# Hybrid decoder layer on one core: norm row first, the first two token tiles ahead of the value weights and multiplied together, other small work moved

## The reference

```
hn   = rms_norm(x, g_pre_mix)
proj = hn @ w_in                      # 3078 columns: q, k, v of 6 MoBA heads, q, k, v of 6 forgetting heads,
                                      # 6 forget logits, 3 x 256 conv channels
moba = block attention, own 256-token block causal, plus past blocks, with a relative bias rel_bias[bucket(dist), head]
fox  = softmax(q k / 8 + cum[t] - cum[s], causal) v,   cum = cumsum(log_sigmoid(f_logit + b_f))
conv = gate_b * causal_conv3(gate_c * h)
mixed = concat(moba, fox, conv) @ w_out
x    = x + rms_norm(mixed, g_post_mix)
h2   = rms_norm(x, g_pre_ffn)
ff   = (silu(h2 @ w_gate) * (h2 @ w_up)) @ w_down      # inner width 2816
out  = x + rms_norm(ff, g_post_ffn)
```

## Time and profile before

| | us |
|---|---|
| three runs | 581.50, 582.97, 585.07 |
| their median | 582.97 |
| the profiled execution | 584.72 |
| its span, first to last instruction | 583.0 |
| TensorE busy (weight loads) | 572.5 (505.7) |
| VectorE, ScalarE, GpSimd busy | 471.9, 320.5, 117.3 |

### The profile page before, as it was taken

How to read it: one execution, slowest core, us unless ns; L and a number is a source line. 1 busy time by engine, 2 the same in 40 slices (tenths; PEclk the granted TensorE clock), 3 DMA queues, 4 the chain that set the end, 5 groups by cost and what they waited for, 6 DMA issues and landing times.

```text
span 583.0 us, 9681 instructions
## 1 busy us (share of the span) xinstructions
PE 572.5 (98%) x3380; PEld 505.7 (87%) x3380; DVE 471.9 (81%) x790; ACT 320.5 (55%) x539; POOL 117.3 (20%) x128
## 2 busy tenths in 40 slices
PE   8999999999999998999999999999999999999996
PEld 5988788888888887899999999999999988888884
DVE  2756888888787954589989888988898778898787
ACT  3644666566565643656454545545463565547752
POOL 3011100113220010000322324242323004344100
PEclk9999999999999998999999999999999999999999
DMA  8254343337312481122142323223231449999843
GB/s 331 74 180 147 98 117 112 92 108 232 107 43 78 144 319 73 63 83 74 72 146 73 128 87 131 85 79 137 81 135 72 144 154 285 262 213 206 161 144 144
DMA packets 27624, 78.92 MB, mean 135 GB/s; under 512 B 2972, under 2 KB 2972, under 8 KB 27594
## 3 DMA queue, kind: packets, MB, share of 16 engines
q1 hardware_dynamic: 18492, 56.92, 27.8%
q0 software_dynamic: 9008, 21.53, 16.8%
q10 hardware_dynamic: 94, 0.09, 0.0%
HBM read 71.16 MB, written 4.22 MB: 129 GB/s over the span
## 4 chain that ended last, share of the span: by engine, by line
PE 91%; DVE 4%; ACT 2%; DMA 1%; issue 1%; POOL 0%; DVEq 0%; ACTq 0%; POOLq 0%
PE bank L1644 9%; PE bank L1646 8%; PE bank L1645 8%; PE bank L1922 8%; PE bank L1921 8%; PE bank L1920 8%; PE bank L1928 6%; PE bank L1986 6%; PE bank L1990 6%; PE bank L1988 6%; PE bank L1697 3%; PE bank L1931 3%; PE bank L1798 2%; PE bank L1786 2%; DMA raw<-in_w_up_units 1%; PE bank L1776 1%
## 5 line engine op out<-in xcount | busy, mean ns | idle before, releaser
L1921 PE MATMUL bank<-tok_lo,form_hi 128*128 128x256 f32 x320 | 90.6, 283 | 0.0
L1922 PE MATMUL bank<-tok_hi,form_lo 128*128 128x256 f32 x320 | 90.6, 283 | 0.0
L1920 PE MATMUL bank<-tok_hi,form_hi 128*128 128x256 f32 x320 | 90.5, 283 | 0.0
L1644 PE MATMUL bank<-hn,w_hi 128*128 128x512 f32 (+1 forms) x200 | 76.7, 384 | 0.6 <-DVE q_hl L1182 0.6
L1646 PE MATMUL bank<-hn,w_lo 128*128 128x512 f32 (+1 forms) x200 | 74.9, 375 | 0.0
L1645 PE MATMUL bank<-hn,w_hi 128*128 128x512 f32 (+1 forms) x200 | 74.7, 373 | 0.0
L1920 PEld LDWEIGHTS bank<-tok_hi,form_hi 128*128 128x128 f32 x320 | 60.9, 190 | 1.9
L1922 PEld LDWEIGHTS bank<-tok_hi,form_lo 128*128 128x128 f32 x320 | 61.1, 191 | 0.0
L1921 PEld LDWEIGHTS bank<-tok_lo,form_hi 128*128 128x128 f32 x320 | 61.0, 191 | 0.0
L1986 PE MATMUL bank<-dw_hi,da_hi 128*128 128x512 f32 x154 | 59.9, 389 | 0.0
L1990 PE MATMUL bank<-dw_hi,da_lo 128*128 128x512 f32 x154 | 59.9, 389 | 0.0
(11 more groups left out here) (204 smaller groups left out, 1411.5 us busy)
## 6 DMA issues: line engine op xcount, KB each, us to landing
raw<-in_w_gate_units SPq DMA_DIRECT2D x22, 512.0 KB, 3.7
raw<-in_w_up_units SPq DMA_DIRECT2D x22, 512.0 KB, 4.5
raw<-in_w_in_units SPq DMA_DIRECT2D x21, 512.0 KB, 3.3
down_x<-in_w_down POOLq DMA_DIRECT2D x15, 512.0 KB, 11.4
down_y<-in_w_down SPq DMA_DIRECT2D x10, 512.0 KB, 11.3
raw<-in_w_out SPq DMA_DIRECT2D x8, 512.0 KB, 3.2
q_lh<-q_hl POOLq DMA_DIRECT2D x12, 256.0 KB, 2.8
down_x<-in_w_down SPq DMA_DIRECT2D x5, 512.0 KB, 4.2
```

What stands on the lines that cost most here:

```text
L1644: nc.tensor.matmul(out_ap, sh, mh, start=first, stop=False)
L1920: nc.tensor.matmul(out_ap, sh, mh, start=first and k == 0, stop=False, skip_group_check=True)
L1921: nc.tensor.matmul(out_ap, sh, ml, start=False, stop=False, skip_group_check=True)
L1922: mm = nc.tensor.matmul(out_ap, sl, mh, start=False, stop=k == HK - 1, skip_group_check=True)
```

## The change

- SyncE loads x tile 1 directly behind x tile 0, ahead of all value weights.
- TensorE: four warm-up transposes instead of twelve ahead of the norm row; the norm row signals after each half, and VectorE's first tile waits for each half apart. The relative rows leave their place ahead of the first turn and stand behind the token rests of tile 0, in PSUM banks 2 and 3. Tiles 0 and 1 are both turned first; then the value product goes part by part through both tiles.
- ScalarE and VectorE take both tiles' squares, normalisation and turns first; ScalarE's copies of the relative rows come after both `tokens_hi`.
- Forget gate: the first sum moves on VectorE from step 2 to 6, the absolute value to 7, exponent and logarithm on ScalarE from step 4 to 9, the running sum from 6 to 11; GpSimd's DMA of it from behind the swap of pair 1 to behind that of pair 2.
- The split of unit U_GU + 1 moves, on ScalarE and VectorE, from before the first mix tile to behind h2 of that tile.

```
-REL_BANKS = (1, 5)
-WARM = (12, 2)
+REL_BANKS = (2, 3)
+WARM = (4, 2)
...
             load_open(0)
+            load_open(1)
             load_values(0)
             load_values(1)
-            load_open(1)
             load_values(2)
...
-                if p == 1:
+                if p == 2:
                     pool.wait_ge(f_cum_done, 1)
...
             squares_of(0)
+            squares_of(1)
             tokens_hi(0)
-            squares_of(1)
+            tokens_hi(1)
             act_e.wait_ge(rel_done, 1)
...
-            tokens_hi(1)
             squares_of(2)
...
-                if g == 4:
+                if g == 9:
                     forget_log()
...
             split(U_GU)
-            split(U_GU + 1)
             nc.scalar.preload_act_table(ACT.Sqrt)
...
                 sum_squares(SQ3, t, x_sb[:, t, :], mix_sq[:, :])
+                if t == 0:
+                    split(U_GU + 1)
...
-                dve.wait_ge(g_done, 1)
                 for b in range(2):
                     c = slice(SEQ * b, SEQ * (b + 1))
+                    if t == 0:
+                        dve.wait_ge(g_done, b + 1)
...
             normalise(0)
+            normalise(1)
+            tokens_lo(0)
             split(0)
-            tokens_lo(0)
-            normalise(1)
+            tokens_lo(1)
             split(1)
             split(2)
-            tokens_lo(1)
             normalise(2)
...
-                if g == 2:
+                if g == 6:
+                    forget_rows_in()
+                if g == 7:
                     forget_z()
-                if g == 6:
+                if g == 11:
                     forget_cum()
...
             split(U_GU)
-            split(U_GU + 1)
...
                                                ).then_inc(h2_done, 1)
+                if t == 0:
+                    split(U_GU + 1)
...
             warm(WARM[0])
             norm_weights()
-            relative_rows()
             warm(WARM[1])
             turn(0)
-            v_rounded(0)
+            turn(1)
+            v_rounded(0, [0])
+            v_rounded(1, [0])
+            v_rounded(0, [1])
+            v_rounded(1, [1])
             v_weight_rests(0, [0])
+            v_weight_rests(1, [0])
+            v_rounded(0, [2])
+            v_rounded(1, [2])
             v_token_rests(0)
-            turn(1)
-            v_rounded(1)
+            relative_rows()
+            v_token_rests(1)
             v_weight_rests(0, [1, 2]).then_inc(proj_done, 1)
-            v_token_rests(1)
             turn(2)
-            v_weight_rests(1, [0, 1, 2]).then_inc(proj_done, 1)
+            v_weight_rests(1, [1, 2]).then_inc(proj_done, 1)
```

More of the change, by code:

```diff
@@ L1185, in evac_lo, with forget_rows_in @@
                     last.then_inc(proj_read, 1)
-            def forget_z():
+            def forget_rows_in():
                 dve.wait_ge(f_rows_done, 1)
@@ L1192, in forget_z @@
                                         ).then_inc(f_z_part, 1)
+            def forget_z():
                 dve.wait_ge(f_z_part, 1)
@@ L1658, in norm_weights @@
                 for b in range(2):
-                    mm = nc.tensor.matmul(bank[:, G_BANKS[b], :], f_one[0:1, 0:P], g_row[:, SEQ * b:SEQ * (b + 1)],
-                                          start=True, stop=True)
-                mm.then_inc(g_done, 1)
+                    nc.tensor.matmul(bank[:, G_BANKS[b], :], f_one[0:1, 0:P], g_row[:, SEQ * b:SEQ * (b + 1)],
+                                     start=True, stop=True).then_inc(g_done, 1)
             def relative_rows():
@@ L1671, in turn @@
             def turn(t):
-                if t == 1:
+                if t == 2:
                     pe.wait_ge(rel_copied, 2)
-                if t >= 2:
+                if t == 3:
                     pe.wait_ge(hn_lo_done, 2 * (t - 2) + 2)
@@ L1698, in v_mm, with v_rounded @@
                                         weight[:, k, :], start=start, stop=stop)
-            def v_rounded(t):
-                for u, (k0, k1) in enumerate(V_CHUNKS):
+            def v_rounded(t, chunks=range(V_UNITS)):
+                for u in chunks:
                     pe.wait_ge(wv_hi_done, u + 1)
-                    for k in range(k0, k1):
+                    for k in range(*V_CHUNKS[u]):
                         if k % 4 == 0:
```

## The result

| | before | after |
|---|---|---|
| median (4 runs of each, alternating) | 583.48 us | 579.52 us (579.3 to 579.92) |
| ratio, 95% interval | | 0.9936 [0.9908, 0.9963] |
| profiled execution, span | 584.72, 583.0 | 579.92, 578.2 |

Predicted were 578.7 us and 0.7% less; measured is 0.6% less.

What follows compares the result with a forecast made beforehand. TensorE, at 98% of the span, was taken to bound the kernel. The terms -3.9 - 0.8 + 0.4 = -4.3 us, taken off the median of 582.97, gave 578.7 us, 0.7% less; range 575.3 to 582.6 us.

Steps and rivals of the forecast that it cites:

- Part 1: Output projection: deferring the weight split removes TensorE's wait for h2 and the low clock behind it, 3.9 us gained.
- Its two halves: Output projection: the removed wait returns 2.17 us, and half of 3.4 us at the low clock returns 1.7.
- Part 2: Opening: value matmuls start at 10.4 instead of 12.89 us; 0.8 us gained at the first projection.
- walk: Opening, timed step by step: clock rise at 14.5 us, about 1 us wait before the third turn, 0.8 us gained.
- bound of 2.4: Opening's best case: clock up at 13.5 us and no wait, 2.4 us gained; the worst case was 1.8 lost.
- Part 3: Early attention: moving the forget gate returns 0.95 us, costs 0.2 and 1.2; sum +0.4 us, bounds -1.1 and +2.1.
- the log's 0.2: Early attention: exponent and logarithm on ScalarE at step 9 cost between 0 and 1.2 us, taken as 0.2.
- "on top" and "idle": Running sum of 1.85 us at step 11: some 0.6 fills VectorE's idle time, 1.2 comes on top.
- Rival A: Output projection: the wait only changes its cause, h2's gain row landing later than 215.3; 581 us, chance 0.14.
- C: Opening: the clock stays low through the 72 value matmuls of three tiles; slower, 587 us, chance 0.07.
- D: Opening: tile 1's x late, the tiles hardly run together, the opening gives nothing; 579.5 us, inside the forecast's 0.62.
- B: Everything returns: opening 2.4, forget gate's move 1.1, with the split's 3.9 in all -7.4; 575.6 us, chance 0.17.

Runs made afterwards that it cites:

- experiment 1: Kernel before with only the second weight split moved behind h2 of mix tile 0: 577.47 us (6 runs), ratio 0.9924.
- 9: Kernel before with only the second weight split moved behind h2 of mix tile 0, measured a second time: 580.38 us (12 runs), ratio 0.9980.
- experiment 11: Changed kernel with the forget gate back in its old places (deferred split and new opening stay): 579.62 us (12 runs), ratio 0.9977.
- experiment 4: Kernel before with 16 identity transposes filling TensorE's wait ahead of h2 of tile 0: 584.05 us (one run).
- experiment 5: Changed kernel with the second weight split back in its old place ahead of the mix: 581.04 us (12 runs), ratio 0.9974.
- 3: Kernel before with only the forget gate's operations moved: 581.86 us (10 runs), ratio 0.9984.
- 2: Kernel before with only the opening changed: 582.29 us (10 runs), ratio 1.0000.
- second series: Changed kernel measured again with no edit: 579.69 us (11 runs), ratio 0.9950.
- experiment 7: Changed kernel with the third tile's sum of squares on ScalarE ahead of its wait for the relative rows: 579.26 us (10 runs), ratio 0.9952.
- third series: Changed kernel measured a third time with no edit: 579.77 us (12 runs), ratio 0.9964.
- experiment 8: Changed kernel with the third sum of squares early and the running sum at step 14 instead of 11: 578.69 us (12 runs), ratio 0.9931.

## Why the prediction was right or wrong

Sign and total were right: 578.7 us predicted, 579.5 to 579.8 measured in three series. Its terms were not all right, and in the profiled pair two errors cancelled, the opening's larger gain and the loss in the down projection. That the total came out is partly luck.

**Part 1, 3.9 us.** Right to 0.1 against the profiled execution: 3.92, 3.93, 3.94 and 3.96 us across the mix in experiments 1 and 9, the changed kernel and experiment 11. Its two halves hold for that execution as well: 1.55 us for the clock (forecast 1.7, experiment 4) leave 2.4 for the wait (2.2). But that execution was not the usual one. Where the raw unit lands earlier and the clock stays up, the split is worth only 1.4 to 1.8 (changed kernel less 5; 1 less 3; 11 less 2). Of the other 2.2 to 2.6 us, 1.55 are paid only when the clock falls, and 0.6 to 1.0 only when the unit is as late as there. **The step that failed is the use of that sum for the median.** I took 4.3 us off the median of 582.97 although the profiled execution, at 584.72, lay 1.75 above it. All 95 runs of the kernel before lie in three groups:

| group, us | runs | median |
|---|---|---|
| 578.6 to 580.3 | 23 | 579.3 |
| 580.7 to 583.3 | 49 | 582.0 |
| 584.0 to 586.1 | 23 | 584.8 |

The profile before is in the last: late rise of the clock and a fall behind the gap. That the groups are these two draws is argued from one profile of the last and from the shifts of experiments 1 and 3 (3.6 us for an early rise, 2.2 for no fall; 584.8 less either is 581.2 or 582.6, less both 579.0), not shown for each run. Experiment 4 warns against it: its one run, with the clock up at the gap, took 584.05 us. What is shown: with the split removed from the path, the last group is gone. None of the 18 runs of experiments 1 and 9 is above 581.2.

Over all runs the kernel before has a mean of 582.05 us and the changed one (27 runs) 579.59: 2.5 us less. By the same count the split alone has 579.49 (18 runs). It carries most of the change; that it carries all of it is not shown. Its two series lie 4.2 and 1.35 us below the kernel before that ran beside them, by the means, and the kernel without it (experiment 5) still lies 0.9 below.

**Part 2, 0.8 us.** Value matmuls from 10.27 (walk: 10.4), the wait before the third turn and its releaser, all as walked. In the profile the term was 3.04 instead of 0.8, beyond its bound of 2.4, by one step: the rise taken at 14.5. That time also holds a slip. I added the 5.1 us behind the first turn to 10.4, where the walk's turns end; its first turn starts at 7.0, which gives 12.1 and not 15.5. The middle of 12.1 and 13.5 is 12.8, and at 12.7 the rise came in two of the three profiles of the changed kernel, with 1.87 us gained. Rises at 10.2 and 12.7 us gave 3.04 and 1.87, 0.46 us for each microsecond; carried on to 14.5 that gives 1.0, an estimate that supports the walk. But the rise is a draw, made anew in each execution. In eight profiles with the new opening it came at 9.6 to 12.7 us; with the old one at 5.2, 14.7, 15.8, 15.9, 16.1 and 16.7. The old opening, with its dozen warm-up transposes, seems to draw 5 us now and then and 15 mostly, the new one neither. The times fit this without proving it: opening_only's series is level with before, and 11 is 0.4 us below 9 by the means (579.73 and 580.10), a difference uncertain by 0.8. What the opening is worth on average stays open between nothing and about 1 us. I had made its 2.4 and -1.8 us bounds of one execution's walk where they were bounds of a draw. The Trainium skill ("TensorE: Matmul & The Clock Gate", Part 1) says that the number of matmuls run at the low clock differs between runs of one kernel; the rises above agree, at 10.2, 12.7 and 12.7 us in the three profiles of the changed kernel.

**Part 3, +0.4 us.** Measured -0.1: step 4 returned 0.84 (forecast 0.95), step 12 took 1.03 (forecast 1.2), the log's 0.2 was nothing, and the steps between gained 0.27 that the forecast did not have. The transfer by "on top" and "idle" was sound.

**What was not forecast.** The down projection gave back 2.3 us in the profile of the changed kernel. Rival A (a late gain row) did not occur, nor C or D; B's opening did, by the clock. Behind the mix the profile stood at 7.1 us gained, near B's 7.4; with nothing given back that execution would have taken 577.6 us, still 2 us above B's 575.6, which had been taken off the median too.

**What stays open** is why it is given back. In eight profiles the two down_x loads that go out ahead of the first down_y were issued before 467 us, and seven of them gave back 0.8 to 2.3 us. In the six where they went out later (467.4 and on), nothing was. The exception among the eight, experiment 1, issued them earliest, at 465.3. It is also the only one of the eight with the old opening; but the opening alone (5.39 us early) gave back nothing.

One thing goes along with it that no run varied by itself. The views of the DMA queues list a single 16 KB packet of instructions in this stretch; in the changed kernel, 464 to 480 us (queue and kind, packets, MB, share of 16 engines):

```profile
q8 instruction: 1, 0.02, 0.5%
```

The same window of the kernel before has none on this queue. In all eight profiles with the new opening it comes within 0.1 us ahead of one of SyncE's load issues, and the issue behind that one follows only 1.3 to 1.6 us later, where it usually follows after 0.5. In the changed kernel, its second series and experiments 5, 7 and 11 this is the second down_x load: it takes 5.1 to 7.6 us to land, and 1.5 to 2.3 us are given back. In the third series, in 8 and in 2 it is the first down_y: the down_x load takes its usual 4.3 to 4.5, and 1.3, 0.8 and 0 are given back. None of the six profiles with the old opening has such a packet there, and none gave anything back, experiment 1 included. So the packet, whose place in the stream the new opening may have moved, is a rival to the early issue as the cause; neither is shown.

The rate of the loads in three-microsecond windows, in the changed kernel and in that of experiment 1:

```profile
469.00:472.00 3.00, 3.00 (x15) 2.49 (x14) 1.90 (x2) 3.00 (x3) 0.24 (x1) 1.00 0.62 160
472.00:475.00 3.00, 3.00 (x15) 2.49 (x14) 2.12 (x2) 1.47 (x2) 0.00 (x0) 1.00 0.99 288
```

```profile
469.00:472.00 3.00, 3.00 (x15) 2.49 (x14) 1.43 (x2) 3.00 (x2) 0.00 (x0) 1.00 0.80 253
472.00:475.00 3.00, 3.00 (x15) 2.49 (x14) 2.58 (x2) 1.96 (x3) 1.39 (x2) 1.00 1.05 411
```

The same transfers run at 160 and 253 GB/s. Both windows follow the start of the broadcast of g_post_ffn (128 copies of one row, POOL's queue), as a shallower dip does in the kernel before and in experiments 2 and 9. The loads that are late there do not catch up; that the stream of down weights is the limit from then on is my reading, not shown. Moving that broadcast away was not tried.

The best kernel of the study is that of experiment 8: 578.69 us, 0.9931.

## What to carry to other kernels

Before a sum made from one execution is taken off a median, place that execution among the times of the others: one that lies high has paid for something that the median run does not pay, and a term that removes it is worth only its share of the runs. A stall at the end of a chain that hangs on one transfer is as long as that transfer is late, and it can have a second price, a lower clock behind it: 1.55 us here behind 2.17 us of idle time, nothing behind 1.54, 1.50 and 1.14. And when a wait is removed by reordering one engine's queue, look at what stood behind it there: in experiment 7 the wait went and one of 0.75 us came back five matmuls later.

## Unexpected in the hardware

TensorE's clock fell behind an idle gap of 2.17 us, and not behind gaps of 1.54, 1.50 and 1.14 us in the same place, one profile each; whether the length alone decides is not shown. In experiment 1 TensorE ran at the pace of 2.4 GHz from 5.2 us, then the clock read 0.50 from 8.7 to 12.0 with TensorE busy for all of these 3.3 us and of the 4.6 before, then 1.00 again: being busy did not keep the clock up there. A 256 KB load of down weights took 4.3 to 4.5 us in nine profiles, 5.1 in one and 6.6 to 7.6 in four, of nearly the same work.
